# The second norm by halves of the tokens, with the third layer's first weights split early

## The reference

```python
h = rmsnorm(x, ffn1_pre_norm[l])
x = x + 0.5 * rmsnorm(swiglu(h, w_ffn1_in[l], w_ffn1_out[l]), ffn1_post_norm[l])   # first layer

h = rmsnorm(x, mix_pre_norm[l])
y = hybrid_mixer(h, w_in[l], ...)       # attention and a gated recurrence; ends with y @ w_out
x = x + rmsnorm(y, mix_post_norm[l])    # the second norm, "post2"

h = rmsnorm(x, ffn2_pre_norm[l])        # "pre3"
x = x + 0.5 * rmsnorm(swiglu(h, w_ffn2_in[l], w_ffn2_out[l]), ffn2_post_norm[l])   # third layer

# rmsnorm(x, g) = x * rsqrt(mean(x * x) + 1e-6) * g
# swiglu(x, w_in, w_out): gate, up = split(x @ w_in); (silu(gate) * up) @ w_out
```

## Time and profile before

| | us |
|---|---|
| median of 3 runs | 1489.06 (1487.78 to 1489.80) |
| the profiled execution | 1489.92 |
| its span, first to last instruction | 1488.1 |
| PE busy | 1477.8 (99%) |
| DVE busy | 722.7 (49%) |
| ACT busy | 586.4 (39%) |

### The profile page before, as it was taken

How to read it: one execution, slowest core, us unless ns; L and a number is a source line. 1 busy time by engine, 2 the same in 40 slices (tenths; PEclk the granted TensorE clock), 3 DMA queues, 4 the chain that set the end, 5 groups by cost and what they waited for, 6 DMA issues and landing times.

```text
span 1488.1 us, 20133 instructions
## 1 busy us (share of the span) xinstructions
PE 1477.8 (99%) x7516; PEld 1221.5 (82%) x7516; DVE 722.7 (49%) x1153; ACT 586.4 (39%) x940; POOL 20.1 (1%) x35
## 2 busy tenths in 40 slices
PE   9999999999999999999999999999999999999998
PEld 7888888887898888888888888888878888888886
DVE  6444444223763455454246665654347444444223
ACT  5233233223432555553254654553344332233122
POOL 0000000000100000000000000000000000000000
PEclk9999999999999999999999999999999999999999
DMA  5322223332332222222322222223331222322332
GB/s 192 99 96 90 96 99 99 99 97 89 120 102 91 88 72 89 71 60 97 99 86 71 71 72 70 72 68 99 100 116 68 87 97 99 98 89 95 100 99 99
DMA packets 39397, 137.68 MB, mean 93 GB/s; under 512 B 4743, under 2 KB 4743, under 8 KB 39344
## 3 DMA queue, kind: packets, MB, share of 16 engines
q1 hardware_dynamic: 37728, 132.14, 27.4%
q0 software_dynamic: 1472, 4.76, 1.2%
q10 hardware_dynamic: 144, 0.04, 0.0%
HBM read 134.00 MB, written 2.13 MB: 91 GB/s over the span
## 4 chain that ended last, share of the span: by engine, by line
PE 96%; DVE 1%; ACT 1%; DMA 1%; issue 0%; SPq 0%; DVEq 0%; ACTq 0%
PE ps L290 27%; PE ps L291 27%; PE ps L292 27%; PE ps L872 1%; PE ps L874 1%; PE ps L873 1%; PE ps L1158 1%; PE ps L1138 1%; PE ps L1037 1%; PE ps L1038 1%; PE ps L1036 1%; PE ps L1518 1%; PE ps L1535 1%; PE ps L1123 1%; PE ps L1541 1%; PE ps L1505 1%
## 5 line engine op out<-in xcount | busy, mean ns | idle before, releaser
L269 ACT ACTIVATE whi<-raw 128x1024 fp32r<-128x1024 f32 x238 | 251.9, 1059 | 615.4 <-PE ps L292 553.9
L290 PE MATMUL ps<-hh,whi 128*128 128x512 f32 x1248 | 492.0, 394 | 1.8 <-DVE hl L748 1.0
L291 PE MATMUL ps<-hl,whi 128*128 128x512 f32 x1248 | 486.2, 390 | 0.0
L292 PE MATMUL ps<-hh,wlo 128*128 128x512 f32 x1248 | 485.9, 389 | 0.0
L274 DVE TENSOR_TENSOR wlo<-raw,whi 128x1024 fp32r<-128x1024 f32 x238 | 291.5, 1225 | 394.5 <-ACT whi L269 394.2
L290 PEld LDWEIGHTS ps<-hh,whi 128*128 128x128 f32 x1248 | 234.2, 188 | 55.8 <-issue 2.9
L292 PEld LDWEIGHTS ps<-hh,wlo 128*128 128x128 f32 x1248 | 234.3, 188 | 49.5
L291 PEld LDWEIGHTS ps<-hl,whi 128*128 128x128 f32 x1248 | 234.4, 188 | 46.9 <-issue 0.2
L451 DVE TENSOR_TENSOR tmp<-ps,rstd 128x512 f32<-128x512 f32 x44 | 30.4, 690 | 121.3 <-PE ps L292 121.3
L290 PE MATMUL ps<-whi,ah 128*128 128x512 f32 x176 | 68.5, 389 | 0.0
L292 PE MATMUL ps<-whi,al 128*128 128x512 f32 x176 | 68.5, 389 | 0.0
(11 more groups left out here) (269 smaller groups left out, 1748.3 us busy)
## 6 DMA issues: line engine op xcount, KB each, us to landing
raw<-in_wstream SPq DMA_DIRECT2D x242, 512.0 KB, 3.3
xt<-in_x_t SPq DMA_DIRECT2D x8, 256.0 KB, 5.7
out<-out_tok SPq DMA_DIRECT2D x8, 256.0 KB, 2.0
bias<-vec_dram POOLq DMA_DIRECT2D x8, 192.0 KB, 3.2
raw<-in_wstream SPq DMA_DIRECT2D x4, 256.0 KB, 4.7
bias<-vec_dram POOLq DMA_DIRECT2D x8, 128.0 KB, 3.3
v_mid<-v_tok POOLq DMA_DIRECT2D x2, 384.0 KB, 4.5
cst<-in_consts POOLq DMA_DIRECT2D x1, 640.0 KB, 5.8
```

The source lines that it names most:

```text
L269: nc.scalar.activation(whi[:, s, :], raw[:, s, :], ACT.Copy).then_inc(head_done, 1)
L290: nc.tensor.matmul(out, w, m, start=start, stop=False)
L291: nc.tensor.matmul(out, w, ml, start=False, stop=False)
L292: return nc.tensor.matmul(out, wl, m, start=False, stop=stop)
```

## The change

- The last two columns of the output projection (6 and 7) are computed in two halves of 256 tokens: column 6 and 7 for the first half, then 6 and 7 for the second. All steps of the norm behind them (squares, sum, Ln, Exp, scaled, added, hh, hl) are done by halves too, and so are the first two pairs of the third layer.
- The sum for the first half stands inside column 6's second half, the one for the second half inside the third layer's first half. Column 7's squares are now added by DVE. The 24 unread matmuls are gone.
- The third layer's first two pairs are split early, into `whi_x` and a new `whi_y`; their blocks stand in the stream behind columns 0 and 1, and behind 2 and 3. The third pair goes to `whi` behind columns 6 and 7.
- The sum of squares for the third layer's own `rstd` stands behind the first projection of the third pair, not ahead of it.
- Beside these, the semaphore `first_head` of the first layer is counted on `half_split` instead, with the waits raised to match.

The diff, cut to its core. `leave` is the square and the gained copy of one column, `gained_half` the hh of ACT or the hl of DVE for one half, `scaled` and `added` the old steps on 256 tokens.

```diff
-        at[0] = arena + 4 * S * (FT - KT)
+        at[0] = arena + 4 * S * (FT - 2 * KT)
+        whi_y = place("whi_y", [P, 2, BLK], F32R)
+        wlo_y = place("wlo_y", [P, 2, BLK], F32R)
...
+        def head_in(act, high, pair, s):
+
+            act.wait_ge(raw_in[s], 16 * pair + 32)
+            nc.scalar.activation(high[:, s, :], raw[:, s, :], ACT.Copy).then_inc(head_done, 1)
+
+        def tail_in(dve, high, low, pair, s):
+
+            dve.wait_ge(head_done, 2 * pair + s + 3)
+            nc.vector.tensor_tensor(low[:, s, :], raw[:, s, :], high[:, s, :].bitcast(F32),
+                                    ALU.subtract).then_inc(split_done, 1)
...
-            order = [(kt, j) for kt in range(KT - 2) for j in (1, 0)]
-            order += [(kt, j) for j in (0, 1) for kt in (KT - 2, KT - 1)]
-            for kt, j in order:
-                pe.wait_ge(*counted("pre3", "ready", kt + 1))
-                for s in range(2):
-                    if kt == 0:
-                        pe.wait_ge(split_done, 2 * first + 2 * (1 - j) + s + 1)
-                    high, low = ((whi, wlo), (whi_x, wlo_x))[j]
-                    last = product(ps[:, 2 * j + s, :], high[:, s, kt * P:kt * P + P], low[:, s, kt * P:kt * P + P],
-                                   hh[:, kt, :], hl[:, kt, :], kt == 0, kt == KT - 1)
-                    if kt == KT - 1:
-                        last.then_inc(block_done, 1)
...
+            plain = [(kt, j) for kt in range(KT) for j in (1, 0)]
+            ends = [(kt, j) for kt in range(KT - 2) for j in (1, 0)]
+            ends += [(kt, j) for j in (0, 1) for kt in (KT - 2, KT - 1)]
+            for half, order in enumerate((plain, ends)):
+                cols = TOKENS[half]
+                for i, (kt, j) in enumerate(order):
+                    pe.wait_ge(*counted("pre3", "ready", KT * half + kt + 1))
+                    if half == 0 and i == 4:
+                        pe.wait_ge(*counted("post2", "acc", KT + 1))
+                        nc.tensor.matmul(ps[:, 6, TOKENS[1]], ones[:], y0[:, TOKENS[1]], start=True, stop=True
+                                         ).then_inc(norm_sem("post2", "sum"), 1)
+                    for s in range(2):
+                        if half == 0 and kt == 0:
+                            pe.wait_ge(split_done, 2 * (first - 1 - 2 * j) + s + 1)
+                        high, low = ((whi_y, wlo_y), (whi_x, wlo_x))[j]
+                        tile = slice(kt * P, kt * P + P)
+                        last = product(ps[:, 2 * j + s, cols], high[:, s, tile], low[:, s, tile], hh[:, kt, cols],
+                                       hl[:, kt, cols], kt == 0, kt == KT - 1)
+                        if half == 1 and kt == KT - 1:
+                            last.then_inc(block_done, 1)
+            project(pe, first + 2, 0, ps[:, 5, :], hh, hl)
             pe.wait_ge(*counted("pre3", "acc", KT - 1))
             nc.tensor.matmul(ps[:, 4, :], ones[:], y0[:], start=True, stop=True).then_inc(norm_sem("pre", "sum"), 1)
-            project(pe, first + 2, 0, ps[:, 5, :], hh, hl)
...
-            head(act, first + 1, 0, 2 * first + 1)
-            if n == 3:
-                head(act, first + 1, 1, 2 * first + 2)
+            if n == 1:
+                head(act, first + 1, 0, 2 * first + 1)
...
+        TOKENS = (slice(0, S // 2), slice(S // 2, S))
+
+        def w_out_pair(d):
+            return FIRST["w_out"] + (0, 2, 4, 5)[d // 2]
+
+        def w_out_bank(d, half):
+            return (6, 7, 4, 5)[d - 6 + 2 * half] if d >= 6 else 4 + d % 4
+
+        def w_out_pe(pe):
+            first = FIRST["w_out"]
+
+            def column(d, half, cols):
+                for k in range(KT):
+                    if d == 0:
+                        pe.wait_ge(sem("yl_done"), k + 1)
+                    if half == 1 and d == KT - 2 and k == 4:
+                        pe.wait_ge(*counted("post2", "acc", KT - 1))
+                        nc.tensor.matmul(ps[:, 0, TOKENS[0]], ones[:], y0[:, TOKENS[0]], start=True, stop=True
+                                         ).then_inc(norm_sem("post2", "sum"), 1)
+                    last = product(ps[:, w_out_bank(d, half), cols], *wcols(d % 2, k * P), yh[:, k, cols],
+                                   yl[:, k, cols], k == 0, k == KT - 1)
+                return last
+
+            for d in range(KT - 2):
+                pe.wait_ge(split_done, 2 * w_out_pair(d) + d % 2 + 1)
+                if d >= 4:
+                    pe.wait_ge(*counted("post2", "left", d - 3))
+                column(d, 0, slice(0, S)).then_inc(block_done, 1)
+            for half in range(2):
+                for d in (KT - 2, KT - 1):
+                    if half == 0:
+                        pe.wait_ge(split_done, 2 * w_out_pair(d) + d % 2 + 1)
+                    pe.wait_ge(*counted("post2", "left", d - 3 + 2 * half))
+                    column(d, half, TOKENS[half]).then_inc(block_done if half else sem("half_column"), 1)
...
+        def half_rstd_act(act, half):
+
+            act.wait_ge(*counted("post2", "sum", half + 1))
+            nc.scalar.activation(rstd[:, TOKENS[half]], ps[:, (0, 6)[half], TOKENS[half]], ACT.Ln, scale=1.0 / D,
+                                 bias=eps[:]).then_inc(norm_sem("post2", "rstd"), 1)
+            act.wait_ge(*counted("post2", "rstd", 2 * half + 1))
+            nc.scalar.activation(rstd[:, TOKENS[half]], rstd[:, TOKENS[half]], ACT.Exp, scale=-0.5
+                                 ).then_inc(norm_sem("post2", "rstd"), 1)
...
+            act.wait_ge(block_done, 2 * first)
+            head_x(act, first, 0)
+            head_x(act, first, 1)
+            for d in range(KT - 2):
+                act.wait_ge(block_done, 2 * first + d + 1)
+                if d >= 2:
+                    act.wait_ge(*counted("post2", "acc", max(1, d - 2)))
+                leave(d, 0, slice(0, S))
+                if d < 2:
+                    head(act, first + 1, d, 2 * first + d + 1)
+                    if d == 1:
+                        head_in(act, whi_y, first + 2, 0)
+                        head_in(act, whi_y, first + 2, 1)
+                else:
+                    head(act, first + 3 + (d - 2) // 2, d % 2, 2 * first + d + 1)
+            for d in (KT - 2, KT - 1):
+                act.wait_ge(sem("half_column"), d - 5)
+                act.wait_ge(*counted("post2", "acc", d - 2))
+                leave(d, 0, TOKENS[0])
+            half_rstd_act(act, 0)
+            act.wait_ge(block_done, 2 * first + KT - 1)
+            leave(KT - 2, 1, TOKENS[1])
+            for d in range(3):
+                gained_half(d, 0)
+            act.wait_ge(block_done, 2 * first + KT)
+            leave(KT - 1, 1, TOKENS[1])
+            for d in range(3, 6):
+                gained_half(d, 0)
+            half_rstd_act(act, 1)
+            for d in range(6, KT):
+                gained_half(d, 0)
+            head(act, first + 5, 0, 2 * first + KT - 1)
+            gained_half(0, 1)
+            gained_half(1, 1)
+            head(act, first + 5, 1, 2 * first + KT)
+            for d in range(2, KT):
+                gained_half(d, 1)
+                square_pre3(act, d - 2)
+            square_pre3(act, KT - 2)
+            square_pre3(act, KT - 1)
...
+            tail_x(dve, first, 0)
+            tail_x(dve, first, 1)
+            for d in range(KT - 2):
+                if d == 1:
+                    dve.wait_ge(*counted("post2", "sq", 2))
+                    nc.vector.tensor_tensor(y0[:], sq[:, 0, :], sq[:, 1, :], ALU.add).then_inc(norm_sem("post2", "acc"), 1)
+                elif d > 1:
+                    dve.wait_ge(*counted("post2", "sq", d + 1))
+                    dve.wait_ge(*counted("post2", "acc", d - 1))
+                    nc.vector.tensor_tensor(y0[:], y0[:], sq[:, d % 2, :], ALU.add).then_inc(norm_sem("post2", "acc"), 1)
+                if d < 2:
+                    tail(dve, first + 1, d)
+                    if d == 1:
+                        tail_in(dve, whi_y, wlo_y, first + 2, 0)
+                        tail_in(dve, whi_y, wlo_y, first + 2, 1)
+                else:
+                    tail(dve, first + 3 + (d - 2) // 2, d % 2)
+            acc_half(6, 0)
+            acc_half(7, 0)
+            for half in range(2):
+                for d in range(KT):
+                    scaled(d, half)
+                    if half == 0 and d in (2, 4):
+                        acc_half((6, 7)[d == 4], 1)
+                    if d >= 1:
+                        gained_half(d - 1, half)
+                    added(d, half)
+                gained_half(KT - 1, half)
+                tail(dve, first + 5, half)
...
-            columns_pe(pe, "w_out", "post2", KT, yh, yl, sem("yl_done"), 0)
-            pe.wait_ge(*counted("post2", "left", KT - 1))
-            pe.wait_ge(*counted("post2", "last", 1))
-            for _ in range(24):
```

(67 more changed lines are left out.)

51 lines of the change are left out of this document (23 added, 28 removed).

## The result

| | us |
|---|---|
| before, median of 7 runs | 1489.36 |
| changed kernel, median of 7 runs | 1494.52 (1493.39 to 1495.27) |
| ratio | 1.0038, 95% interval 1.0028 to 1.0047 |
| its profiled execution / span | 1494.19 / 1492.4 |

The kernel is slower by 5.2 us in the medians. Forecast were 3.4 us more and 1492.5, within 1488.0 to 1495.8.

A forecast was written before the change was run, and what follows sets the result against it. TensorE (PE) was taken to bound the kernel, with 96% of the chain. -5.5 + 2.1 + 0.85 + 0.5 + 0.45 + 3.8 gave +2.2, the clock +1.2: +3.4 on 1489.06, 1492.5 us, range 1488.0 to 1495.8.

The forecast's parts named there:

- waits of columns 2 and 4: Output projection: PE stalls 1.2 us and 0.9 us because slot 0 of the raw buffer delivers weights late.
- column 7's wait: Output projection: column 7's weights need whi[1], free only when column 5 is done; PE stalls 0.85 us.
- wait between halves, at the end: Third layer's first two pairs: PE waits 0.5 us for the second half's first hl, 0.45 in its last groups.
- PE's own work: Output projection to fourth pair: 79.8 us of PE work instead of 85.3, 5.5 less, with 256-token matmuls at 0.120.
- The norm by halves: Second norm: its loop takes 1.40 us a tile against PE's 1.44, so it holds within a half, by little.
- The moved sum: Third layer's rstd sum behind the third pair's first projection: fourth pair's weights come late, PE stalls 3.8 us with restart.
- Together 2.1: Output projection: the summed stalls for weights of columns 2 and 4, 2.1 us, with loads of 3.4 us.
- The clock: Behind the stall ahead of the fourth pair: the granted clock falls, costing 1.2 us beyond the idle time.
- (a): Rival, behind the fourth pair's stall: as forecast but the clock stays; +2.2 us, 1491.3; chance 0.29.
- (b): Rival, output projection: early blocks come in time, the 2.1 us of columns 2 and 4 go; +0.1, 1489.2; chance 0.10.
- (c): Rival, fourth pair: its late tail is hidden and the moved sum costs nothing; -1.6 us, 1487.5; chance 0.08.
- (d): Rival, halved columns and pairs: 256-token matmuls held by their loads at 0.140; about +7 us, 1496; chance 0.13.

The follow-up runs named there:

- f1: Changed kernel plus 15 matmuls that nobody reads, in PE's idle time ahead of the fourth pair; 1493.64 us, ratio 1.0030 to before.
- f4: Kernel before with only the sum for the third layer's rstd moved behind the third pair's first projection; 1493.64 us, ratio 1.0031 to before.
- g3: Changed kernel with the sum for the third layer's rstd put back ahead of the third pair's first projection; 1495.38 us, ratio 1.0047 to before.
- f2: Changed kernel with the fourth pair's weights split earlier, block 0 ahead of Ln and Exp, block 1 behind the second silu; 1490.23 us, ratio 1.0011 to before.
- f3: Changed kernel with the two extra pairs later in the stream, behind columns 2 and 3 and behind 4 and 5; 1492.72 us, ratio 1.0032 to before.

## Why the prediction was right, and where it was off

Counted from the output projection's start, where the prediction has 1066.54:

| step | predicted | measured |
|---|---|---|
| a matmul of 256 | 0.120 | 0.120 |
| waits of columns 2 and 4 | 1.2 + 0.9 | 1.2 + 2.5 |
| column 7's wait | 0.85 | 0.76 |
| third layer starts | 47.6 | 49.4 |
| two pairs end | 72.0 | 73.8 |
| one tile of the norm's loop | 1.40 | 1.40 |
| wait between halves, at the end | 0.5, 0.45 | 0.3, 0.3 |
| VectorE's adds end | 76.3 | 78.0 |
| sum for rstd | 77.4 | 79.3 |
| from the sum to the fourth pair | 10.1 | 10.1 |
| fourth pair | 87.5 | 89.4 |
| clock | +1.2 | +1.3 (f1) |

- **PE's own work** was sized from two rows that don't have the operation, a 512-column matmul and a load, and their spacing came out exactly. By the formula of the Trainium skill ("TensorE: Matmul & The Clock Gate", section "Back-to-back issue gap"), which the page gives for a single, isolated matmul, it would be 0.109; the runs, where each matmul has weights of its own, show 0.120.
- **The norm by halves** did what it should: third layer's first half without a wait. One turn of the loop in the changed kernel, added to added, with ACT's hh between, is 1119.14 - 1117.74 = 1.40:

```profile
1117.74 0.41 DVE L719 TENSOR_TENSOR xt<-xt,tmp 128x256 f32<-128x256 f32 x1
...
1118.74 0.48 DVE L725 SCALAR_TENSOR_TENSOR hl<-xt,par,hh 128x256 fp32r<-128x256 f32 x1 [0.24 <-ACT hh L646]
1119.14 0.42 DVE L719 TENSOR_TENSOR xt<-xt,tmp 128x256 f32<-128x256 f32 x1
...
1118.19 0.51 ACT L646 ACTIVATE hh<-xt,par 128x256 fp32r<-128x256 f32 x1 [0.89 <-DVE xt L719]
```

  The price of the halves shows on VectorE: it needs 25.3 us for the sixteen half tiles, with one weight tail and two late adds among them (1111.48 to 1136.73), and needed 18.0 for the eight whole ones (1114.40 to 1132.38). So the adds of the squares end 78.0 us after the output projection's start, against 71.2 before:

```profile
1138.57 4.67 DVE L762 TENSOR_TENSOR y<-y,sq_all 128x512 f32<-128x512 f32 x6
```

- **The moved sum** was the largest term. f4 shows its price in the kernel before; g3 shows that in the changed kernel it can't be had back, since the sum then waits for those adds. What is fixed is the chain from the adds to the fourth pair's weights, and f2 shows that taking the weights out of it does help. The chain behind the sum, answering to the earlier trace rows: Ln at 1145.57, table load, second silu at 1151.62, head, tail to 1154.45, 9.94 us behind 1144.51, as before.

```profile
1145.57 0.69 ACT L893 ACTIVATE rstd<-ps,eps 128x512 f32<-128x512 f32 x1 [7.79 <-PE ps L384]
1146.29 0.63 ACT L896 ACTIVATE rstd<-rstd 128x512 f32<-128x512 f32 x1
1146.94 1.28 ACT L432 ACT_TABLE_LOAD   x1
...
1151.62 0.63 ACT L416 ACTIVATE silu<-tmp 128x512 f32<-128x512 f32 x1 [1.36 <-DVE tmp L461]
1152.15 1.04 ACT L271 ACTIVATE whi<-raw 128x1024 fp32r<-128x1024 f32 x1
...
1153.22 1.23 DVE L276 TENSOR_TENSOR wlo<-raw,whi 128x1024 fp32r<-128x1024 f32 x1 [1.04 <-ACT whi L271]
```

- **The step that was mis-sized** is "Together 2.1": it measured 3.7. Column 2's 1.2 was right. Column 4's was predicted at 0.9 with all loads at 3.4, and whi_y's first block took 4.9. The prediction names this case beside its sum ("A load of 5.2 on slot 0 would add 1.8") and leaves it out of it. What made it late, as far as seen: a packet of queue 8, "instruction", passed while it was under way. The first fence is the one load issued from 1075 to 1079 and its time to landing, the second that queue between 1077 and 1083.

```profile
raw<-in_wstream SPq DMA_DIRECT2D x1, 512.0 KB, 4.9
```

```profile
q8 instruction: 1, 0.02, 1.1%
```

  In the kernel before, the 5.2 us of the earlier trace rows is a load issued at 1075.81, with such a packet at 1078.9 beside it and no other load in flight. So the earlier trace rows held the number and the trace the hour, and the prediction took the median where the row's maximum lay at this very place. It is no accident of one execution: in all nine traces a packet of that queue comes between 1076.4 and 1079.8, and the load under way takes 4.2 to 5.2 us. Of the 242 loads of the kernel before, 17 take over 4.1 us; 15 of these meet such a packet, the other two have another load in flight. But 15 further loads meet one and take less. That the packet causes the delay was not tried.
- **The clock** fell as forecast, and costs 1.3 to 1.6 us. f2 adds what the prediction did not see: the clock can fall behind a wait of 2.24 us, so in the traced execution its fall stood at a shorter wait once the long stall was gone. In the changed kernel and in f1 the same wait was longer (2.31 and 2.48 us), and the clock stayed at 1.00 behind it, so the length of the wait alone does not decide; what does is open.
- Sum with measured terms: -5.5 + 3.7 + 0.8 + 0.6 + 3.8 + 1.5 = +4.9, against 5.6 in the stretch and 5.2 in the medians. Of the difference of the stretch, 4.1 stand ahead of the fourth pair and 1.5 behind it. The 0.7 that is missing can be read from PE's timeline: behind each of the five waits ahead of the rstd sum, PE takes another 0.10 to 0.14 us before the usual spacing holds (0.6 in all), and the second half sum held PE 0.56 instead of 0.43. The prediction puts both at nothing. Its +3.4 is so 2.2 short of the stretch's 5.6: 1.6 for column 4, 0.7 for these and 0.3 for the clock, less 0.4 for waits of column 7 and the halves that were shorter than forecast.
- Of the rivals, (a), the clock that stays, fell with the 0.50 behind the stall; (b) would have needed column 4 in time, and it was 2.5 late; (c) fell with f4; (d) with the 0.120.

## What to carry to other kernels

When a step is moved behind another to hide its own wait, measure the distance from it to the next thing that depends on it, weights in a shared staging buffer included, and count what is left to cover that distance; here one moved line alone costs the kernel before about what the whole change lost, and putting it back into the changed kernel wins nothing, since VectorE's adds end 6.8 us later there. What helped was to split the weights outside that chain (f2). A gap on TensorE can have two prices, the idle time and the clock behind it, and when one gap is closed the second can turn up at another (once, in f2), so gaps are best closed together. And a prefetch that fits by the median time of a load does not fit if the row's maximum falls at its place.

## What the runs showed of the hardware

- Matmuls with 128 x 128 loads each: 0.227 us apart for 512 columns, 0.120 for 256. A 512-column matmul that is made into two of 256 takes 13 ns more, 1.9 us for the 144 here.
- After idle times of 3.58 (changed kernel, f3, f4), 4.10 (g3) and once 2.24 us (f2) the granted clock fell to the lower of its two levels (1.2 GHz): the stretches of 3.1 to 3.8 us behind them have a mean of 0.50 to 0.57. After 2.31 us (changed kernel), 2.48 us (f1) and 1.96 us (g3, at column 4) it did not fall. Filler matmuls in the gap kept it at 1.00 (f1).
- VectorE's adds of 128x256 took 0.42 us, as in the earlier trace rows; its hl 0.48 and ScalarE's hh 0.51, as worked out from the slopes between wider instructions.
- Most 512 KB loads took 3.1 to 3.5 us. The one issued 9 to 12 us into the output projection, which met an instruction packet in each of the nine traces, took 4.2 to 5.2 us; two in the changed kernel that met none, but were issued while another load was in flight, took 4.2.
